# Laying the prompt rows out by feature for the input projection, and the output product ahead of a tile's first projection group

## The reference

```python
mod = silu(c) @ w_ada + b_ada                  # -> shift, scale, gate, twice
h = rmsnorm(x, g_mix) * (1 + sc_m) + sh_m      # the change is in how h is made
u = h @ w_in                                   # 1024 x 3072: conv_a | conv_b | q | k | v | g
glu = a * sigmoid(b); conv = depthwise(glu, width 31); conv_out = silu(layernorm(conv))
q, k = rotary(q), rotary(k); o, state = retention(q, k, v, state)   # chunks of 128 rows
ret_out = groupnorm(o) * silu(g)
x = x + gt_m * (concat[conv_out, ret_out] @ w_out)
h = rmsnorm(x, g_ffn) * (1 + sc_f) + sh_f
x = x + gt_f * (shared_expert(h) + top-6 of 64 routed experts(h))
y = rmsnorm(x, g_final)
```

## Time and profile before

| | |
|---|---|
| median of 3 runs | 1590.01 us (1589.70 to 1591.05) |
| the profiled execution, its own time | 1590.49 us |
| its span in the profile | 1588.7 us |
| PE busy | 1444.5 us, 91% of the span |
| DVE busy | 845.3 us, 53% |
| ACT, POOL busy | 213.0 us, 494.7 us |
| mean granted clock of TensorE | 0.958 |

### The profile page before, as it was taken

How to read it: one execution, slowest core, us unless ns; L and a number is a source line. 1 busy time by engine, 2 the same in 40 slices (tenths; PEclk the granted TensorE clock), 3 DMA queues, 4 the chain that set the end, 5 groups by cost and what they waited for, 6 DMA issues and landing times.

```text
span 1588.7 us, 17546 instructions
## 1 busy us (share of the span) xinstructions
PE 1444.5 (91%) x5851; PEld 653.0 (41%) x5851; DVE 845.3 (53%) x2135; ACT 213.0 (13%) x358; POOL 494.7 (31%) x426
## 2 busy tenths in 40 slices
PE   4899999999999999988799998999979999999947
PEld 2344454555545455554343332344423333333313
DVE  1147778998988999575533323333333232333317
ACT  1111231312222231222000000000000000000003
POOL 0001010121211111304545444454544545454410
PEclk9999999999999999958799999999999999999978
DMA  9987211211120000603399999999999999999975
GB/s 333 329 316 266 96 43 67 82 40 70 40 83 27 32 29 27 189 33 114 119 369 326 344 370 360 364 373 364 373 366 358 375 363 374 353 368 360 372 219 239
DMA packets 93690, 370.17 MB, mean 233 GB/s; under 512 B 17763, under 2 KB 29447, under 8 KB 68461
## 3 DMA queue, kind: packets, MB, share of 16 engines
q1 hardware_dynamic: 69637, 304.77, 49.5%
q0 software_dynamic: 23968, 64.35, 16.2%
...
## 4 chain that ended last, share of the span: by engine, by line
DMA 37%; PE 30%; DVE 19%; issue 7%; SPq 4%; ACT 2%; POOL 1%; POOLq 0%; DVEq 0%; ACTq 0%
DMA acc_rows<-W,kT 17%; DMA acc_rows<-xr,kT 15%; PE U L649 9%; PE R L702 8%; DVE cv L1188 7%; PE U L831 5%; PE R L847 2%; SPq L396 2%; DMA W<-in_w_ada 2%; DMA acc_rows<-xr,shared_f 1%; DMA W<-h_rows,q_r 1%; PE R L613 1%; SPq L403 1%; PE U L673 1%; PE U L757 1%
## 5 line engine op out<-in xcount | busy, mean ns | idle before, releaser
L649 PE MATMUL U<-W,hT 128*128 128x512 f32 x864 | 386.2, 601 | 1.2 <-issue 1.2
L1188 DVE SCALAR_TENSOR_TENSOR cv<-win,cw,cv 128x128 f32<-128x128 f32 x960 | 254.8, 344 | 1.4
L831 PE MATMUL U<-W,cat 128*32 128x512 f32 (+2 forms) x1072 | 239.0, 614 | 5.8 <-issue 3.7
L831 PE MATMUL U<-W,hT 128*32 128x512 f32 (+2 forms) x976 | 237.9, 608 | 6.0 <-issue 6.0
L847 PE MATMUL R<-W,glu 128*32 128x512 f32 (+2 forms) x1024 | 240.8, 597 | 1.3 <-DVE glu L1458 1.3
L649 PEld LDWEIGHTS U<-W,hT 128*128 128x128 f32 x864 | 162.5, 193 | 189.0 <-issue 189.0
L1445 DVE STREAM_TRANSPOSE cat<-W 128x1024 f32<-128x1024 f32 x33 | 67.4, 2042 | 203.0 <-DMA W<-h_rows,q_r 200.1
L1445 DVE STREAM_TRANSPOSE hT<-x_t 128x1024 f32<-128x1024 f32 x33 | 67.3, 2039 | 189.5 <-DMA x_t<-h_rows,q_r 168.0
L847 PEld LDWEIGHTS R<-W,glu 128*32 128x32 f32 (+2 forms) x1024 | 84.1, 138 | 150.8 <-issue 149.3
L831 PEld LDWEIGHTS U<-W,hT 128*32 128x32 f32 (+2 forms) x976 | 88.5, 144 | 131.2 <-issue 129.7
L831 PEld LDWEIGHTS U<-W,cat 128*32 128x32 f32 (+2 forms) x1072 | 85.4, 139 | 135.1 <-issue 130.9
...
## 6 DMA issues: line engine op xcount, KB each, us to landing
W<-in_w SPq DMA_DIRECT2D x192, 1024.0 KB, 17.6
W<-in_w_ada SPq DMA_DIRECT2D x24, 1024.0 KB, 8.7
...
W<-acc_rows SPq DMA_DIRECT2D x16, 512.0 KB, 9.5
x_rows<-xr SPq DMA_DIRECT2D x9, 512.0 KB, 3.3
h_rows<-xr SPq DMA_DIRECT2D x9, 512.0 KB, 2.7
x_t<-in_x_prompt SPq DMA_DIRECT2D x8, 512.0 KB
...
```

The source lines that it names most:

```text
L649: last = mm(U[BANK[g]][:, :], hT[:, k, :], w_in[:, k, 512 * g:512 * g + 512], start=k == 0, stop=k == KT - 1)
L831: last = mm(U[1][cols, :], xgT[z][:, k, cols], w13[:, :, k, :], start=k == 0, stop=k == KT - 1)
L1188: ins = v.scalar_tensor_tensor(cv[:, c, :], win[:, c, w:w + P], cw[:, c, w:w + 1], cv[:, c, :], ALU.mult, ALU.add)
```

## The change

The host also gives the prompt turned: `x_prompt_t` holds, for each tile, the features on the rows and the 128 tokens of each eighth of the features side by side, so that a plain load of 128 rows of 4 KB gives `hT` unscaled. SP loads it straight into `hT` (`load_turned`), as soon as GK has read the tile before (uk_done). Scaling is done there: PE spreads 1/std over the partitions by one product of 128x128 into `X` (`spread_std`), DVE multiplies `hT` by it (`scale_turned`, one instruction at the head of the turn), and ACT applies scale and shift per feature, which is now per partition, by eight instructions of 128x128 (`hT_scale`). The columns `A_col` and `B_col` come from two transposes of each vector (`turn_vector`) and take the place of rows made by four products each. `x_t` serves the sum of squares only, for the prompt; DVE's scaling by `A_m` and POOL's `shift` stay for the sample tile alone, as do `x_trans` and `hT_copy`. On PE, `positions`, the transposes of k_r and `mix_out` come ahead of GB; on ACT, the copy to `kT` and `hT_scale` come ahead of the sigmoid.

```diff
             sp.dma_start(x_t[:, :], t["x_prompt"][0, 0:P, :]).then_inc(x_in, 16)
+            sp.dma_start(hT[:, :, :], t["x_prompt_t"][0:P].rearrange("p (k n) -> p k n", k=KT)).then_inc(xT_in, 16)
...
             def load_next(i):
-                sp.wait_ge(x_posed, i + 1)
+                sp.wait_ge(norm1_ssq, i + 1)
...
+            def load_turned(i):
+                sp.wait_ge(uk_done, i + 1)
+                sp.dma_start(hT[:, :, :], t["x_prompt_t"][bass.ds((i + 1) * P, P)].rearrange("p (k n) -> p k n", k=KT)).then_inc(xT_in, 16)
...
-            for p in range(8, 19):
+            for p in range(8, 15):
+                load_ada(p)
+            load_turned(0)
+            for p in range(15, 19):
                 load_ada(p)
...
                 load_residual(i - 1)
+                load_turned(i)
                 load_rope(i)
...
-            def spread_row(x, outs):
+            def turn_vector(x):
                 pe.wait_ge(mod_ready, x + 1)
-                for j in range(4):
-                    last = mm(outs[j // 2][:, 256 * (j % 2):256 * (j % 2) + 256], ident[:, 32 * j:32 * j + 1].to_broadcast([P, P]),
-                              ada_part[x][:, :], start=True, stop=True)
+                for half in range(2):
+                    last = tr(U[x][:, P * half:P * half + P], ada_part[x][:, P * half:P * half + P], ident[:, :])
                 last.then_inc(ab_posed, 1)
+
+            def spread_std(i):
+                pe.wait_ge(h_scaled, i + 1)
+                pe.wait_ge(h2T_ready, floor(i - 2))
+                mm(X[:, 0:P], rstd1.to_broadcast([P, P]), ident[:, :], start=True, stop=True).then_inc(x_posed, 1)
...
                     four(q_r, q_posed, win_ready, j + 1, q_rot, j + 1)
+                if place:
+                    positions(m - 2, pick, i - 1)
+                if tail:
+                    four(k_r, k_posed, qT_ready, j + 1, k_rot, j + 1)
+                if route:
+                    mix_out(m)
                 if front:
                     pe.wait_ge(hT_ready, i + 1)
                     project(i, GB, ub_done, sg_ready, i)
-                if place:
-                    positions(m - 2, pick, i - 1)
-                if route:
-                    mix_out(m)
-                if tail:
-                    four(k_r, k_posed, qT_ready, j + 1, k_rot, j + 1)
...
-                if nxt:
-                    x_trans(i + 1)
+                if nxt and isinstance(i, int) and i + 1 == TP:
+                    x_trans(TP)
+                elif nxt:
+                    spread_std(i + 1)
...
+            def hT_scale(i):
+                act.wait_ge(h_ready, i + 1)
+                act.wait_ge(ab_ready, 2)
+                for k in range(KT):
+                    last = nc.scalar.activation(hT[:, k, :], hT[:, k, :], ACT.Identity, scale=A_col[:, k:k + 1], bias=B_col[:, k:k + 1])
+                last.then_inc(hT_ready, 1)
+                act.wait_ge(hT_ready, i + 1)
...
+            def scale_turned(i):
+                dve.wait_ge(x_posed, i + 1)
+                dve.wait_ge(xT_in, 16 * (i + 1))
+                v.tensor_tensor(hT[:, :, :], hT[:, :, :], X[:, 0:P].unsqueeze(1).to_broadcast([P, KT, P]), ALU.mult).then_inc(h_ready, 1)
+                dve.wait_ge(h_ready, i + 1)
...
+                if front and not (isinstance(i, int) and i in (0, TP)):
+                    scale_turned(i)
                 if tail and prompt:
                     dve.wait_ge(win_ready, j + 1)
```

More of the change, by code:

```diff
@@ L809, in _ @@
             body(4)
-            with pe.Fori(5, TP) as i:
+            with pe.Fori(5, TP - 1) as i:
                 body(i)
+            body(TP - 1)
             body(TP, nxt=False)
@@ L993, in body @@
                     act.wait_ge(qT_ready, j + 1)
+                if tail:
+                    act.wait_ge(k_posed, j + 1)
+                    nc.scalar.activation(kT[:, :, :], T4, ACT.Copy).then_inc(kT_ready, 1)
+                    act.wait_ge(kT_ready, j + 1)
+                if front and not (isinstance(i, int) and i == TP):
+                    hT_scale(i)
                 if front:
@@ L1055, in body @@
                     act.wait_ge(catB_ready, j + 1)
-                if nxt:
-                    hT_copy(i + 1)
+                if nxt and isinstance(i, int) and i + 1 == TP:
+                    hT_copy(TP)
                 if front:
@@ L1064, in _ @@
             norm1(0)
-            act.wait_ge(ab_posed, 1)
-            nc.scalar.activation(A_m, X[:, :], ACT.Copy).then_inc(ab_ready, 1)
-            act.wait_ge(ab_posed, 2)
-            for c in range(2):
-                nc.scalar.activation(B_m[:, 512 * c:512 * c + 512], U[c][:, :], ACT.Copy).then_inc(ab_ready, 1)
-            hT_copy(0)
+            for x, col in enumerate((A_col, B_col)):
+                act.wait_ge(ab_posed, x + 1)
+                nc.scalar.activation(col.rearrange("p (j z) -> p j z", z=2), U[x][:, 0:2 * P].rearrange("p (z j r) -> p j z r", z=2, j=4)[:, :, :, 0],
+                                     ACT.Copy).then_inc(ab_ready, 1)
+            act.wait_ge(ab_ready, 2)
             body(0, tail=False, route=False)
@@ L1074, in _ @@
             body(3)
-            with act.Fori(4, TP) as i:
+            with act.Fori(4, TP - 1) as i:
                 body(i)
+            body(TP - 1)
             body(TP, nxt=False)
@@ L1135, in norm1 @@
                 dve.wait_ge(norm1_std, i + 1)
-                link(v.reciprocal(rstd1, std1))
+                dve.wait_ge(x_posed, i)
                 if isinstance(i, int) and i == TP:
+                    link(v.reciprocal(rstd1[0:NS, :], std1[0:NS, :]))
                     dve.wait_ge(smod1_in, 32)
-                v.scalar_tensor_tensor(x_t[:, :], x_t[:, :], rstd1, A_m, ALU.mult, ALU.mult).then_inc(h_scaled, 1)
+                    v.scalar_tensor_tensor(x_t[0:NS, :], x_t[0:NS, :], rstd1[0:NS, :], A_m[0:NS, :], ALU.mult, ALU.mult).then_inc(h_scaled, 1)
+                else:
+                    v.reciprocal(rstd1, std1).then_inc(h_scaled, 1)
                 dve.wait_ge(h_scaled, i + 1)
+            def scale_turned(i):
[3 more added lines that the diff above has]
+                dve.wait_ge(h_ready, i + 1)
             def ada_vector(x):
@@ L1156, in _ @@
             ada_vector(0)
-            dve.wait_ge(ab_ready, 1)
             norm1(0)
+            scale_turned(0)
             ada_vector(1)
@@ L1579, in shift @@
                 pool.wait_ge(h_scaled, i + 1)
-                g_.tensor_tensor(x_t[:, :], x_t[:, :], B_m, ALU.add).then_inc(h_ready, 1)
+                g_.tensor_tensor(x_t[0:NS, :], x_t[0:NS, :], B_m[0:NS, :], ALU.add).then_inc(h_ready, 1)
             def ret_out(j):
@@ L1597, in fill_list @@
                                             oob_is_err=False).then_inc(slots_out, 16)
-            pool.wait_ge(ab_ready, 3)
-            shift(0)
-            shift(1)
             pool.wait_ge(modv_in, 80)
-            ret_out(0)
-            shift(2)
-            for i in range(2, 4):
-                ret_out(i - 1)
-                shift(i + 1)
+            for j in range(3):
+                ret_out(j)
             pool.wait_ge(table_filled, 16)
             before = own.k
-            with pool.Fori(4, TP) as i:
+            with pool.Fori(4, TP - 1) as i:
                 own.at((i - 4) * POOL_LOOP + before)
@@ L1613, in _ @@
                 ret_out(i - 1)
-                shift(i + 1)
                 assert own.k == POOL_LOOP, own.k
+            own.at(before + (TP - 5) * POOL_LOOP)
+            fill_list(TP - 5)
+            ret_out(TP - 2)
+            shift(TP)
             own.at(before + (TP - 4) * POOL_LOOP)
@@ L1699 @@
 TAPS = (16, 19, 19, 28)
-DVE_LOOP = 155
+DVE_LOOP = 154
 POOL_LOOP = 2
@@ L1755 @@
     arrays |= {name: np.ascontiguousarray(a.astype(np.float32)) for name, a in constants().items()}
+    turned = arrays["x_prompt"][0].reshape(TP, P, KT, P)
+    arrays["x_prompt_t"] = np.ascontiguousarray(turned.transpose(0, 3, 2, 1).reshape(SEQ, D))
     t = {name: nc.dram_tensor("in_" + name, a.shape, F32, kind="ExternalInput").ap() for name, a in arrays.items()}
```

18 lines of the change are left out of this document (8 added, 10 removed).

## The result

The changed kernel takes 1596.05 us (median of 15 runs, 1592.48 to 1599.83), the one before, run beside it, 1589.16 us (15 runs, 1585.03 to 1592.32): 1.0042 times as long, with an interval of 1.0032 to 1.0051. I had forecast 1585.2, with a range up to 1593.0. The change makes the kernel slower. The profiled execution took 1597.56 us by its own clock, its span is 1595.7 us (before 1588.7) and the mean granted clock 0.953 (0.958).

What follows compares the result with a forecast made beforehand. Turns were taken as bound by a ring passing between PE and DVE, the later part by weight streaming. 1.6 + 4.0 - 2.55 - 3.4 - 3.4 - 1.1 = -4.85 us gave 1585.2 us; range 1577.5 to 1593.

Steps and rivals of the forecast that it cites:

- The start: Turn 0: one more 0.52 MB transfer in the queue makes w_ada load 8 land later; +1.6 us.
- Turn 1: GB waits for eight ACT instructions, starting at K + 8.0 (K: end of GK), 4.5 us later; +4.0 us.
- My rival: Clock falls ahead of GG in four turns, with a new gap after q_r; costs 6.8 us, 1592.0; chance 0.10.
- Turns 2 and 3: DVE's longer wait for mix_out goes, with PE limiting the gain to 1.7 us each; -3.4 us.
- PE can use only 1.7 us: Turns 2 and 3: DVE's last tap moves 2.9 us earlier, but PE gains only 1.7 us a turn.
- My third rival: Something taken for hidden feeds DVE, so turns 4 to 8 stay: 1592.2, or 1588.8 with half the savings; chance 0.10.
- Turns 4, 5 and 7: Taps start 1.4 us later, at K + 4.75, but DVE's 2.25 us wait for mix_out goes; -2.55 us.
- the 4.5 us at which I had made it a rival: Turned tile lands late: beyond 4.5 us each further us costs 4.8; 5.6 us gives 1596.6; chance 0.13.
- Turn 6: Relieved DVE begins the taps 1.15 us earlier and loses a wait of about 2.25 us; -3.4 us.
- Turn 8: Sample tile, no turned load: PE gains 1.65 us less a 0.5 us gap; -1.1 us.

Runs made afterwards that it cites:

- f3: Changed kernel with w_ada loads 8 to 11 issued right behind w_in, ahead of the tables; 1590.05 us.
- f1: Changed kernel with seven overwritten products filling PE's wait ahead of GB in turn 1; 1599.59 us.
- e1: Changed kernel with norm2 ahead of the sigmoid of GB on ACT; 1596.31 us.
- e3: Kernel before with only the new order on PE and the kT copy ahead of the sigmoid on ACT, plus norm2 ahead of that sigmoid; 1593.49 us.
- h1: Changed kernel with the edits of f2, f3, f4, g5 and u1, and norm2 ahead of the sigmoid; 1569.68 us.
- h3: As h1, but turned tile 1 is issued ahead of w_ada loads 12 to 14; 1563.28 us.
- f2: Changed kernel with the turned tile loaded a whole turn ahead into a second buffer; 1592.05 us.
- u1: Changed kernel with DVE's turns 5 and 6 written out in place of its loop; 1589.38 us.
- g5: Changed kernel with k_r's transposes behind mix_out on PE and hT_scale ahead of the copy to kT on ACT; 1591.21 us.
- f4: Changed kernel with ada_pairs 12 to 14 moved from behind GK of turn 0 to ahead of GB in turn 1; 1594.31 us.

## Why the prediction was wrong

**The start (+1.6 said, +2.4 measured).** Right: the wait for load 8 ends at 79.56 (I said near 79.5), 1.67 us later than before. I had left out that the wait is then 7.3 us long, and that the pair and GG behind it run slower: 1.94 and 8.68 us in place of 1.57 and 8.28. What I did not see is that the bytes are not all of it: SP issues load 8 only at 73.63 us, behind thirteen tables and eight stores; with it ahead of them the wait is 0.40 us (f3).

**Turn 1 (+4.0 said, +7.1 measured).** The wait itself was right: GB began at K + 7.8, where I had said 8.0. Eight ACT instructions took 3.19 us, where I took 3.5. The estimate by the page of the Trainium skill that I cited (ScalarE: Activation LUTs, What ACT_TABLE_LOAD costs: 386 ns each in a run, 3.2 us) was nearer than the 3.5 us that I took from rows: single ones last 478 ns and overlap. The step that failed is that I priced the wait by its length alone. The missing 3 us are the clock: it falls while PE stands 3.97 us, and GB takes 2.5 us more (f1 shows that it doesn't when the wait is filled); the rest lies in later pairs and their loads. My rival put the falls of the clock ahead of GG; here it came in the wait ahead of GB, and in turn 8 behind the pair of gaps at the head.

**Turns 2 and 3 (-3.4 said, -1.5 measured).** Here the argument failed: "PE can use only 1.7 us" took DVE's path as free of ACT. My third rival allowed for something of the kind, but in turns 4 to 8, and without saying what. I followed who waits for GB on PE, and not what is queued behind the sigmoid on ACT. norm2's root came 1.9 us late (1.88 in turn 2). Mended (e1) the two turns win 2.7 us of the 3.4; a wait of 0.5 us before `norm_sum` is left, in e3, h1 and h3 as well.

**Turns 4, 5 and 7 (-2.55 said, -1.5 measured).** Right in mechanism. The taps start at K + 5.06, not 4.75: the load takes 3.5 us, not 3.3. That is 0.3 of the 0.35 us by which each turn misses. f2 shows that the late load is what holds these turns. The rule of the Trainium skill that I quoted, to issue early and wait late, was right, though the transfer was well below the 4.5 us at which I had made it a rival: at 3.5 us it already cost 2.6 us in these turns (f2), and in h1, where it took 10.9 us, it cost 7.4 us of turn 1.

**Turn 6 (-3.4 said, -0.4 measured).** A misreading. The earlier trace rows show 3.54 us with "issue" as the cause, which means that DVE waited for nothing that the profile knows. I called that DVE coming late. It was the jump of DVE's loop (u1), which the change doesn't touch, and it hid the wait for the turned tile as it had hidden the one for `win`: the taps begin at K + 7.4, not K + 4.75. With the wait for `mix_out` gone `norm_sum` still starts 1.2 us earlier behind K than before (54.6 in place of 55.8), but PE has by then stood 4.83 us in place of 2.20, the clock is at 0.50, and `norm_sum` takes 2.05 in place of 1.13 us: 0.9 of the 1.2 us are lost again.

**Turn 8 (-1.1 said, +1.6 measured).** I had counted the new gap at its length and nothing for the clock. Behind that gap stand 1.7 us of slower clock, as in five more of the nine kernels that have it and in none of the seven that don't (g5 among these). PE's wait for the convolution is still 1.10 us, because norm2's root is late here too.

The misses are 3.1 (turn 1), 3.0 (turn 6), 2.7 (turn 8), 1.9 (turns 2, 3), 1.1 (4, 5, 7) and 0.8 us (start), less 0.8 us behind turn 8: together the 11.85 us between -4.85 and +7.0.

What stays open: why the clock falls behind a given gap in one turn and not in its twin. In e3 the same two gaps (1.50 and 0.39 us) slow `mix_out` in turn 5 and not in turn 4; GG is slowed behind a wait of 1.99 us in turn 5 of u1 and not behind 1.85 us in its turn 6. So a part of what e1 and f4 should have won is not settled by these runs. What they do show: behind each of the nineteen waits of PE of 3.96 us or more in turns 1 to 8 of all these kernels the next products ran slow, and where such a wait was filled (f1) or removed (h3), GB ran at its full pace. Behind shorter ones, up to the longest of 3.08 us (g5, turn 5, not slow), both happened.
